# Decay's and rate's first matrices side by side, applied to the input and to the token difference

## The chip, the cores and the metric

The kernel runs on one core of a Trainium2 chip, as one launch. The time is device microseconds of that core, the median of several runs. Engines are named as in the profile: PE is TensorE (PEld its weight loads), DVE is VectorE, ACT is ScalarE, POOL is GpSimd, SP is SyncE, which issues the weight DMAs.

## The reference, cut to what matters

Two layers, an RWKV-7 layer and a differential-attention layer, 512 tokens of width 1024, all in float32. The change touches the beginning of the first layer:

```python
h = rmsnorm(x, norm_g[layer, 0])
h_prev = jnp.pad(h[:, :-1], ((0, 0), (1, 0), (0, 0)))
dx = h_prev - h
xw = h + dx * mix[1]
xa = h + dx * mix[4]
xg = h + dx * mix[5]
...
w_log = -jax.nn.softplus(-(w0 + jnp.tanh(xw @ w1) @ w2)) - 0.5     # decay
a = jax.nn.sigmoid(a0 + (xa @ a1) @ a2)                              # rate
g = jax.nn.sigmoid(xg @ g1) @ g2                                     # gate
```

`w1` and `a1` are 1024 x 64, `g1` is 1024 x 160. Since the mixing vectors act on the 1024 input channels, `xw @ w1` is the same sum as `h @ w1 + dx @ (mix[1][:, None] * w1)`, and likewise for `a1`.

## The kernel before, in words

Activations lie with channels on partitions: X holds h as 8 tiles (k = 0 to 7) of 128 channels x 512 tokens, the kind V_ of St holds the token difference dx in the same tiles. Every dense product is made of three fp32r matmuls: weights and activations are each split in a high part (a copy rounded to fp32r, made by ACT) and a low part (the rest, a subtraction on DVE for activations and on POOL for weights). For an activation tile k, ACT writes xh (`split_high`, L1333) and DVE then xl (`low`, L1840); for a weight block n, ACT writes whi from the raw weights (`high`, L1326) and POOL wlo (`low`, L461 and L464, in two halves of 128 x 1024 for a full block). PE then runs the three products of a tile, L557 (xh with whi), L558 (xl with whi) and L559 (xh with wlo), into a PSUM bank.

Order at the start, which is written out by hand on each engine and held together by semaphores:

- SP loads x, then the raw weights: block 0 (w1, twice side by side, into slot 0 of wraw), block 1 (a1, twice side by side, slot 1), block 2 (g1, slot 0 again, after block 0's low part is made), block 3 (w2 and a2), then the large squares for K, R and V (L371).
- ACT squares x, PE turns x into channel tiles (L581), ACT copies each to X with its norm gain (L1355), POOL takes the difference of neighbouring tokens (L473, semaphore dx), DVE mixes (`mixes`, L1851: dx times a mixing vector plus h, into a slot of tmp), ACT and DVE split the mixed tile.
- There are six mixed inputs in turn: W (decay), A (rate), G (gate), K, R, V. For each, DVE alternates mix and low part, two mixes ahead. The three first feed `dense_block` 0, 1 and 2 on PE: 24 matmuls for W into bank 0, 24 for A into bank 2, 48 for G into banks 0 and 1.
- Between W and A, DVE computes lambda of the second layer's attention (L1871 to L1875, with an exponential on ACT, L1370).
- ACT takes tanh of rows 0 to 63 of bank 0 after block 0 (L1373), and rows 64 to 127 of bank 2 after G's splits (L1377), splits both (L1381, L1382), takes the sigmoid of G's result (L1385), and then evacuates the eight products with w2 and a2 (L1399), one split of K's mixed input behind each pair. K's first dense product (block 4) follows on PE.
- POOL's queue in that stretch: wlo of block 0, eight differences, wlo of block 1 (L464), of block 2 (L461, L464, which also waits for the end of PE's block 0), of block 3, then the squares.

Semaphores that the prediction speaks of: `h_ready` (a tile of X is written), `dx`, `mix_b` (a mixed tile), `x_hi` and `x_ready` (a tile's high and low part), `w_hi` and `w_lo` (a block's), `pe_step` (one per tile of a dense block), `dense_a` (results that ACT has taken), `lora_rdy`. xh and xl have eight tile slots, used again by each input; `split_high` waits on `pe_step` until the tile's last reader is through.

Of the kernel before, what the change touches and what calls it, by code (L numbers as in the profile page):

```python
# [139 lines left out]
def trunk(nc, x, p, norm_g, mlp_w1, mlp_w2, ple_w_up, ple_w_gate, rwkv_mix, rwkv_w_rkvo, rwkv_w0, rwkv_w1,  # L140
# [5 lines left out]
    with ctx:  # L146
# [4 lines left out]
        def at(name, offset, shape, dtype=F32):  # L151
# [107 lines left out]
            h_ready x_edge mix_b x_hi x_ready acc norm_ps norm_rt dense_a dense_v act_link vec_link pool_link  # L259
            lora_hi lora_rdy g_cum dec exps kk_sq kk_ps kk_rt kk_rs kb_ps kn prep  # L260
            bs_mm nl_raw nl_mask inv_ld inv_lk inv_d tdg
# [15 lines left out]
        def vec(c, v):  # L277
            return PV[:, c, v:v + 1]
# [55 lines left out]
        def _(sp):  # L334
# [8 lines left out]
            def load(n, par, parts):  # L343
                for dst, src in parts:
                    sp.dma_start(dst, src).then_inc(raw[par], 16)
# [4 lines left out]
            def cols(r, w, k=CT):  # L350
                return r[:, 0:k * w].rearrange("p (k n) -> p k n", n=w)
# [3 lines left out]

            load(0, 0, [(cols(r0, P)[:, :, 0:64], w1v), (cols(r0, P)[:, :, 64:128], w1v)])
            load(1, 1, [(cols(r1, P)[:, :, 0:64], a1v), (cols(r1, P)[:, :, 64:128], a1v)])
            slot_free(2)
# [192 lines left out]
        def _(pe):  # L551
# [67 lines left out]
            pe.wait_ge(s.h_ready, 3)  # L619
            dense_block(0, 0, 0, 1, X_W)  # L620
            dense_block(1, 1, 1, 1, X_A)
            pe.wait_ge(s.dense_a, 1)
            dense_block(2, 0, 0, 2, X_G)
# [684 lines left out]
        def _(act):  # L1308
# [43 lines left out]
            act.wait_ge(s.par_ev, 1)  # L1352
            for c in range(CT):
                act.wait_ge(s.x_tr, c + 1)
                A(X[:, c, 4:4 + S], pb[c][:, :], ACT.Copy, scale=vec(c, V_N00)).then_inc(s.h_ready, 1)  # L1355
                if c == 3:
                    high(1, 1, slice(0, 1024), True)

            def mix_high(i, k, free):  # L1360
                act.wait_ge(s.mix_b, 8 * i + k + 1)
                split_high(k, tmp[:, mix_place(i, k), :], None, free)
# [4 lines left out]

            mixes(0, None)
            act.wait_ge(s.lam_s, 1)
            A(lamw[:, 2:4], lamw[:, 0:2], ACT.Exp).then_inc(s.lam_e, 1)  # L1370
            mixes(1, 0)
            act.wait_ge(s.pe_step, 8)
            A(rstd[0:64, :], pb[0][0:64, :], ACT.Tanh).then_inc(s.dense_a, 1)  # L1373
            high(2, 0)
            mixes(2, 8 * 1)
            act.wait_ge(s.pe_step, 16)
            A(rstd[64:128, :], pb[2][64:128, :], ACT.Copy).then_inc(s.dense_a, 1)  # L1377
            high(3, 1, slice(0, 1024))
# [425 lines left out]
        def _(dve):  # L1804
# [37 lines left out]
            def mixes(i, mix):  # L1842

                ahead = 2 if i != 4 else 1

                def mixed(k):
                    if i == 0:
                        dve.wait_ge(s.dx, k + 1)
                    if 8 * i + k - 2 * ahead >= 0:
                        dve.wait_ge(s.x_ready, 8 * i + max(k - 2 * ahead, -1) + 1)  # L1850
                    stt(tmp[:, mix_place(i, k), :], St[:, V_, k, :], vec(k, V_MIX + mix), X[:, k, 4:4 + S], ALU.mult, ALU.add)\  # L1851
                        .then_inc(s.mix_b, 1)
                for k in range(ahead):
                    mixed(k)
                for k in range(CT):
                    if k + ahead < CT:
                        mixed(k + ahead)
                    dve.wait_ge(s.mix_b, 8 * i + k + 1)
                    low(k, tmp[:, mix_place(i, k), :], 8 * i + k)
# [7 lines left out]

            mixes(0, MIX_W)

# [6 lines left out]

            mixes(1, MIX_A)
            mixes(2, MIX_G)
# [513 lines left out]
```

## Time and profile before

| | |
|---|---|
| median of 3 runs | 1600.32 us (1599.81 to 1600.70) |
| profiled execution, its own time | 1600.4 us |
| its span in the trace | 1598.5 us |
| mean granted TensorE clock | 0.977 |
| PE busy | 1494.1 us (93%), 9095 matmuls |
| DVE busy | 741.1 us (46%) |
| ACT busy | 590.8 us (37%) |
| POOL busy | 601.3 us (38%) |

### The profile page before, as it was taken

The page shows a single profiled execution, that of the slowest core. Times are in us where ns is not written, and L with a number is a line of the kernel's source. Part 1 is how long each engine was busy: PE and PEld are TensorE (multiplying, and loading weights), DVE is VectorE, ACT ScalarE, POOL GpSimd, SP SyncE. Part 2 cuts the span into 40 slices and gives each one's busy share as a digit, 9 for nine tenths or more (in the row PEclk, how much of TensorE's full clock was granted, in tenths as well). Part 3 has the DMA queues.
Part 4 walks back from the last instruction along what each step waited for, and adds up shares of the span by engine and source line. Part 5 has one row for each costly group of instructions (what it writes and reads, how often), then busy time and mean ns, then how long its engine had stood idle before and what let it go on. Part 6 is the DMA issues. An engine that isn't in the chain of part 4 may idle for free. (4 is left out here: it accounts for less than half of the span.)

```text
span 1598.5 us, 23571 instructions
## 1 busy us (share of the span) xinstructions
PE 1494.1 (93%) x9095; PEld 1176.7 (74%) x9095; DVE 741.1 (46%) x1148; ACT 590.8 (37%) x928; POOL 601.3 (38%) x326
## 2 busy tenths in 40 slices
PE   3798999888999999999999999979999999999998
PEld 3575677775687888888877677745687888888876
DVE  3874888756744310232046773566453300232143
ACT  4655433545332221233153433267342211232252
POOL 4242332323143444443444243334134443434432
PEclk9898999999999999999999999979999999999999
DMA  5121210031023233233322322110022233233231
GB/s 142 53 79 53 80 53 1 4 114 55 25 82 106 81 104 118 81 103 105 105 87 86 126 84 99 55 53 1 19 87 92 92 105 118 80 105 102 82 106 53
DMA packets 123502, 126.97 MB, mean 79 GB/s; under 512 B 8332, under 2 KB 120204, under 8 KB 123416
## 3 DMA queue, kind: packets, MB, share of 16 engines
q1 hardware_dynamic: 122720, 124.51, 24.0%
q8 instruction: 60, 0.98, 0.3%
q0 software_dynamic: 320, 0.66, 0.2%
q10 hardware_dynamic: 376, 0.61, 0.1%
q14 instruction: 26, 0.21, 0.0%
HBM read 123.64 MB, written 2.12 MB: 79 GB/s over the span
## 5 line engine op out<-in xcount | busy, mean ns | idle before, releaser
L461 POOL TENSOR_TENSOR wlo<-wraw,whi 128x1024 fp32r<-128x1024 f32 x108 | 261.1, 2417 | 812.9 <-ACT whi L1326 786.9
L557 PE MATMUL pb<-xh,whi 128*128 128x512 f32 x1184 | 475.5, 402 | 26.3 <-DVE xl L1840 16.1
L559 PE MATMUL pb<-xh,wlo 128*128 128x512 f32 x1184 | 465.0, 393 | 0.0
L558 PE MATMUL pb<-xl,whi 128*128 128x512 f32 x1184 | 464.8, 393 | 0.0
L557 PEld LDWEIGHTS pb<-xh,whi 128*128 128x128 f32 x1184 | 224.3, 189 | 101.7 <-issue 41.8
L1326 ACT ACTIVATE whi<-wraw 128x2048 fp32r<-128x2048 f32 (+1 forms) x111 | 209.2, 1884 | 224.6 <-PE pb L559 224.5
L464 POOL TENSOR_TENSOR wlo<-wraw,whi 128x1024 fp32r<-128x1024 f32 x111 | 275.1, 2478 | 21.4 <-ACT whi L1326 21.4
L558 PEld LDWEIGHTS pb<-xl,whi 128*128 128x128 f32 x1184 | 224.5, 190 | 47.8 <-issue 3.4
L559 PEld LDWEIGHTS pb<-xh,wlo 128*128 128x128 f32 x1184 | 224.4, 189 | 47.8
L557 PE MATMUL pb<-hid_h,whi 128*128 128x512 f32 x512 | 199.3, 389 | 0.0
L558 PE MATMUL pb<-hid_l,whi 128*128 128x512 f32 x512 | 199.2, 389 | 0.0
L559 PE MATMUL pb<-hid_h,wlo 128*128 128x512 f32 x512 | 199.2, 389 | 0.0
L2156 DVE TENSOR_TENSOR X<-X,pb 128x512 f32<-128x512 f32 x40 | 25.7, 684 | 288.1 <-PE pb L559 288.1
L2188 DVE TENSOR_TENSOR tmp<-pb,rstd 128x512 f32<-128x512 f32 x64 | 41.3, 686 | 208.5 <-PE pb L559 208.0
L1639 ACT ACTIVATE hid_h<-tmp 128x512 f32 (+1 forms) x64 | 39.6, 633 | 251.2 <-DVE tmp L2192 251.2
L557 PEld LDWEIGHTS pb<-hid_h,whi 128*128 128x128 f32 x512 | 96.1, 188 | 20.0
L559 PEld LDWEIGHTS pb<-hid_h,wlo 128*128 128x128 f32 x512 | 96.1, 188 | 19.9
L558 PEld LDWEIGHTS pb<-hid_l,whi 128*128 128x128 f32 x512 | 96.1, 188 | 19.8
L2161 DVE SCALAR_TENSOR_TENSOR xl<-X,PV,xh 128x512 fp32r<-128x512 f32 x48 | 55.8, 1222 | 28.3 <-ACT xh L1335 28.3
L1609 ACT ACTIVATE tmp<-X 128x512 f32<-128x512 f32 x40 | 24.2, 627 | 119.9 <-DVE X L2156 119.9
L1840 DVE TENSOR_TENSOR xl<-tmp,xh 128x512 fp32r<-128x512 f32 x64 | 51.7, 818 | 25.0 <-ACT xh L1333 24.9
L1333 ACT ACTIVATE xh<-tmp 128x512 fp32r<-128x512 f32 x64 | 40.1, 632 | 55.9 <-DVE tmp L1851 28.3
(280 smaller groups left out, 1723.4 us busy)
## 6 DMA issues: line engine op xcount, KB each, us to landing
wraw<-in_mlp_w_dram SPq DMA_DIRECT2D x128, 512.0 KB, 4.3
wraw<-in_rwkv_w_rkvo_dram SPq DMA_DIRECT2D x32, 512.0 KB, 4.3
wraw<-in_ple_w_gate_dram SPq DMA_DIRECT2D x16, 512.0 KB, 4.0
xtok<-in_x_dram SPq DMA_DIRECT2D x8, 512.0 KB, 6.3
wraw<-in_w_k_shared_dram SPq DMA_DIRECT2D x8, 512.0 KB, 4.3
wraw<-in_w_v_shared_dram SPq DMA_DIRECT2D x8, 512.0 KB, 3.9
wraw<-in_diff_w_q_dram SPq DMA_DIRECT2D x8, 512.0 KB, 4.3
wraw<-in_diff_w_o_dram SPq DMA_DIRECT2D x8, 512.0 KB, 4.3
```

Of the source, the lines that this page charges most:

```text
L461: pool.tensor_tensor(wlo[:, par, front], wraw[:, par, front], whi[:, par, front].bitcast(F32), ALU.subtract)
L464: pool.tensor_tensor(wlo[:, par, rng], wraw[:, par, rng], whi[:, par, rng].bitcast(F32), ALU.subtract).then_inc(s.w_lo, 1)
L557: mm(o, wh, ah, start=first, stop=False)
L558: mm(o, wh, al, start=False, stop=False)
L559: return mm(o, wl, ah, start=False, stop=last)
L1326: A(whi[:, par, rng], wraw[:, par, rng], ACT.Copy).then_inc(s.w_hi, 1)
L1333: A(xh[:, k, :], src, ACT.Copy).then_inc(s.x_hi, 1)
L1639: A(hid_h[:, bass.ds(4 * i + 2 * h + m, 1), :], tmp[:, 2 + m:3 + m, :], ACT.Copy)\
L1840: tt(xl[:, k, :], src, xh[:, k, :].bitcast(F32), ALU.subtract).then_inc(s.x_ready, 1)
L2156: tt(X[:, c, 0:S], X[:, c, 0:S] if old is None else old, b, ALU.add).then_inc(sem, 1)
L2161: stt(xl[:, k, :], X[:, k, 0:S], vec(k, gain), xh[:, k, :].bitcast(F32), ALU.mult, ALU.subtract)\
L2188: tt(tmp[:, m, :], pb[2 * h + m][:, :], rstd[:, :], ALU.mult).then_inc(s.dense_v, 1)
```

## The change

The two 64-wide matrices are loaded side by side, [w1 | a1], once into slot 0 and once into slot 1 of wraw. DVE multiplies the second copy in place by the mixing vectors (channels are partitions, so the vector is one number for each partition and tile): two instructions of 128 x 8 x 64, semaphore `w_mix`. ACT makes slot 1's high part after that. The activations that meet them are h itself and dx: X_W now stands for the eight tiles of h, X_A for those of dx. Both passes add into one bank, pb[2], rows 0 to 63 for decay and 64 to 127 for rate. The mixed inputs of W and A are no longer made (16 instructions at L1851); G, K, R and V are mixed as before. ACT splits tile c-1 of h between its copies into X, then the eight tiles of dx. Tanh moves behind G's splits.

```diff
@@ -257,7 +257,7 @@
         names = """gnc_in raw0 raw1 w_hi w_lo pe_step cst_in cst2_in x_in0 x_in1 x_in2 x_in3 rows_in hrows_in x2_in p_in lam_in hot_in
             rel_in bvec_out strip_in out_st x_tr x_sq x_rt x_rs x_dg dx par_tr par_ev small_set gains lam_s lam_e
             h_ready x_edge mix_b x_hi x_ready acc norm_ps norm_rt dense_a dense_v act_link vec_link pool_link
-            lora_hi lora_rdy g_cum dec exps kk_sq kk_ps kk_rt kk_rs kb_ps kn prep
+            w_mix lora_hi lora_rdy g_cum dec exps kk_sq kk_ps kk_rt kk_rs kb_ps kn prep
             bs_mm nl_raw nl_mask inv_ld inv_lk inv_d tdg
             x_unit kv_mm kv_ev bt_mm bt_ev lo_ev vz0 vz1 vb0 vb1 ks_mm ll_ev x5_mm xb_ev t5_mm tt_ev
             z_mm0 z_mm1 z_ev0 z_ev1 u_mm0 u_mm1 u_ev0 u_ev1 grown0 grown1 h_ev0 h_ev1
@@ -353,8 +353,8 @@
             a1v = rwkv_a1[0].rearrange("(k p) n -> p k n", p=P)
             g1v = rwkv_g1[0].rearrange("(k p) n -> p k n", p=P)
 
-            load(0, 0, [(cols(r0, P)[:, :, 0:64], w1v), (cols(r0, P)[:, :, 64:128], w1v)])
-            load(1, 1, [(cols(r1, P)[:, :, 0:64], a1v), (cols(r1, P)[:, :, 64:128], a1v)])
+            load(0, 0, [(cols(r0, P)[:, :, 0:64], w1v), (cols(r0, P)[:, :, 64:128], a1v)])
+            load(1, 1, [(cols(r1, P)[:, :, 0:64], w1v), (cols(r1, P)[:, :, 64:128], a1v)])
             slot_free(2)
             load(2, 0, [(cols(r0, 256)[:, :, 0:128], g1v[:, :, 0:128]),
                         (cols(r0, 256)[:, :, 128:256], g1v[:, :, 32:160])])
@@ -617,9 +617,12 @@
 
 
             pe.wait_ge(s.h_ready, 3)
-            dense_block(0, 0, 0, 1, X_W)
-            dense_block(1, 1, 1, 1, X_A)
-            pe.wait_ge(s.dense_a, 1)
+            for n, x_base in ((N_W1, X_W), (N_A1, X_A)):
+                pe.wait_ge(s.w_lo, n + 1)
+                for k in range(CT):
+                    pe.wait_ge(s.x_ready, x_base + k + 1)
+                    three(pb[2][:, :], n, wslice(n, k * P), xs(k), n == N_W1 and k == 0, n == N_A1 and k == CT - 1)\
+                        .then_inc(s.pe_step, 1)
             dense_block(2, 0, 0, 2, X_G)
 
             pe.wait_ge(s.w_lo, 4)
@@ -1350,30 +1353,35 @@
             A(x_rms, x_ss, ACT.Sqrt, bias=eps_n, scale=1.0 / D).then_inc(s.x_rt, 1)
             high(0, 0, slice(0, 1024), True)
             act.wait_ge(s.par_ev, 1)
-            for c in range(CT):
-                act.wait_ge(s.x_tr, c + 1)
-                A(X[:, c, 4:4 + S], pb[c][:, :], ACT.Copy, scale=vec(c, V_N00)).then_inc(s.h_ready, 1)
-                if c == 3:
+            for c in range(CT + 1):
+                if c < CT:
+                    act.wait_ge(s.x_tr, c + 1)
+                    A(X[:, c, 4:4 + S], pb[c][:, :], ACT.Copy, scale=vec(c, V_N00)).then_inc(s.h_ready, 1)
+                if c:
+                    act.wait_ge(s.h_ready, c)
+                    split_high(c - 1, X[:, c - 1, 4:4 + S], None, None)
+                if c == 6:
+                    act.wait_ge(s.w_mix, 2)
                     high(1, 1, slice(0, 1024), True)
+            for k in range(CT):
+                act.wait_ge(s.dx, k + 1)
+                split_high(k, St[:, V_, k, :], None, 0)
 
 
             def mix_high(i, k, free):
-                act.wait_ge(s.mix_b, 8 * i + k + 1)
+                act.wait_ge(s.mix_b, 8 * (i - 2) + k + 1)
                 split_high(k, tmp[:, mix_place(i, k), :], None, free)
 
             def mixes(i, free):
                 for k in range(CT):
                     mix_high(i, k, free)
 
-            mixes(0, None)
+            high(2, 0)
             act.wait_ge(s.lam_s, 1)
             A(lamw[:, 2:4], lamw[:, 0:2], ACT.Exp).then_inc(s.lam_e, 1)
-            mixes(1, 0)
-            act.wait_ge(s.pe_step, 8)
-            A(rstd[0:64, :], pb[0][0:64, :], ACT.Tanh).then_inc(s.dense_a, 1)
-            high(2, 0)
             mixes(2, 8 * 1)
             act.wait_ge(s.pe_step, 16)
+            A(rstd[0:64, :], pb[2][0:64, :], ACT.Tanh).then_inc(s.dense_a, 1)
             A(rstd[64:128, :], pb[2][64:128, :], ACT.Copy).then_inc(s.dense_a, 1)
             high(3, 1, slice(0, 1024))
             act.wait_ge(s.dense_a, 2)
@@ -1844,9 +1852,7 @@
                 ahead = 2 if i != 4 else 1
 
                 def mixed(k):
-                    if i == 0:
-                        dve.wait_ge(s.dx, k + 1)
-                    if 8 * i + k - 2 * ahead >= 0:
+                    if k >= 2 * ahead or i > 2:
                         dve.wait_ge(s.x_ready, 8 * i + max(k - 2 * ahead, -1) + 1)
                     stt(tmp[:, mix_place(i, k), :], St[:, V_, k, :], vec(k, V_MIX + mix), X[:, k, 4:4 + S], ALU.mult, ALU.add)\
                         .then_inc(s.mix_b, 1)
@@ -1855,7 +1861,7 @@
                 for k in range(CT):
                     if k + ahead < CT:
                         mixed(k + ahead)
-                    dve.wait_ge(s.mix_b, 8 * i + k + 1)
+                    dve.wait_ge(s.mix_b, 8 * (i - 2) + k + 1)
                     low(k, tmp[:, mix_place(i, k), :], 8 * i + k)
 
             def lora_low(dst, high, src, r):
@@ -1865,7 +1871,14 @@
                 if z.stop:
                     ts(dst[z], src[z], 0.0, None, ALU.mult).then_inc(s.lora_rdy, 1)
 
-            mixes(0, MIX_W)
+            dve.wait_ge(s.raw1, 32)
+            for m, mix in ((0, MIX_W), (1, MIX_A)):
+                w = wraw[:, 1, 0:CT * P].rearrange("p (k c) -> p k c", c=P)[:, :, 64 * m:64 * m + 64]
+                tt(w, w, PV[:, :, V_MIX + mix:V_MIX + mix + 1].to_broadcast([P, CT, 64]), ALU.mult).then_inc(s.w_mix, 1)
+            for k in range(CT):
+                low(k, X[:, k, 4:4 + S], k)
+            for k in range(CT):
+                low(k, St[:, V_, k, :], CT + k)
 
             dve.wait_ge(s.lam_in, 16)
             link(tt(lrow[:, 0:2, :], lrow[:, 0:4:2, :], lrow[:, 1:4:2, :], ALU.mult))
@@ -1874,7 +1887,6 @@
             link(tt(lamf, lamw[:, 2:3], lamw[:, 3:4], ALU.subtract))
             link(ts(lamf, lamf, LAMBDA_INIT, None, ALU.add))
 
-            mixes(1, MIX_A)
             mixes(2, MIX_G)
             dve.wait_ge(s.lora_hi, 4)
             lora_low(lora_l[:, 0, :], lora_h[:, 0, :], rstd[:, :], slice(0, 64))
```

DVE at the start, from the constants' last instruction to the third mix of G. Before (tmp<-St,PV,X is a mix, xl a low part):

```order
L1831 TENSOR_SCALAR small<-small 128x1
L1851 SCALAR_TENSOR_TENSOR tmp<-St,PV,X 128x512 x3
L1840 TENSOR_TENSOR xl<-tmp,xh 128x512
L1851 SCALAR_TENSOR_TENSOR tmp<-St,PV,X 128x512
...
L1840 TENSOR_TENSOR xl<-tmp,xh 128x512 x3
L1871 TENSOR_TENSOR lrow<-lrow 128x128
L1872 TENSOR_REDUCE small<-lrow 128x2
```

Now:

```order
L1839 TENSOR_SCALAR small<-small 128x1
L1877 TENSOR_TENSOR wraw<-wraw,PV 128x8x64 x2
L1848 TENSOR_TENSOR xl<-X,xh 128x512 x8
L1848 TENSOR_TENSOR xl<-St,xh 128x512 x8
L1884 TENSOR_TENSOR lrow<-lrow 128x128
L1885 TENSOR_REDUCE small<-lrow 128x2
L1887 TENSOR_TENSOR small<-small 128x1
L1888 TENSOR_SCALAR small<-small 128x1
L1857 SCALAR_TENSOR_TENSOR tmp<-St,PV,X 128x512 x3
```

The sixteen mixes of W and A are gone, two products on the weights stand in front, all sixteen low parts come ahead of lambda's four small instructions, and G's mixes follow those.

ACT in the same stretch, from the last copy into whi before the tiles to the lambda exponential. Before:

```order
L1326 ACTIVATE whi<-wraw 128x1024
L1355 ACTIVATE X<-pb,PV 128x512 x4
L1326 ACTIVATE whi<-wraw 128x1024
L1355 ACTIVATE X<-pb,PV 128x512 x4
L1333 ACTIVATE xh<-tmp 128x512 x8
L1370 ACT_TABLE_LOAD
```

Now, from the second copy of slot 1's weights on (ahead of it stand seven copies into X with a split behind each from the second on):

```order
L1329 ACTIVATE whi<-wraw 128x1024
L1359 ACTIVATE X<-pb,PV 128x512
L1336 ACTIVATE xh<-X 128x512 x2
L1336 ACTIVATE xh<-St 128x512 x8
L1329 ACTIVATE whi<-wraw 128x2048
L1381 ACT_TABLE_LOAD
```

Slot 1's high part has moved from behind the fourth copy to behind the seventh, and block 2's (128x2048) from behind A's splits and tanh to ahead of lambda's exponential.

## Rows read from the trace of the kernel before

**Rows 1.** The page: PE's busy time over the whole span.
```profile
PE 1494.1 (93%) x9095; PEld 1176.7 (74%) x9095; DVE 741.1 (46%) x1148; ACT 590.8 (37%) x928; POOL 601.3 (38%) x326
```

**Rows 2.** Stages: start:end, length, busy us by engine, clock, DMA share, GB/s.
```profile
32.40:44.00 11.60, 8.42 (x24) 5.58 (x24) 11.23 (x17) 4.64 (x7) 3.51 (x2) 0.71 0.17 47
...
46.70:55.20 8.50, 7.96 (x24) 4.85 (x24) 8.46 (x14) 5.39 (x8) 0.00 (x0) 0.80 0.01 2
55.20:61.20 6.00, 0.12 (x1) 0.02 (x1) 6.00 (x4) 1.72 (x4) 5.19 (x2) 0.80 0.00 0
61.20:74.30 13.10, 13.09 (x49) 10.62 (x50) 9.52 (x16) 8.40 (x12) 2.40 (x1) 0.83 0.34 108
74.30:92.25 17.95, 14.77 (x50) 10.31 (x48) 14.58 (x17) 16.14 (x27) 6.08 (x2) 0.81 0.30 97
```

**Rows 3.** Timeline of DVE at the start: start us, us, instruction, idle before.
```profile
22.55 0.15 DVE L1831 TENSOR_SCALAR small<-small 128x1 f32<-128x1 f32 x1
...
27.31 1.51 DVE L1851 SCALAR_TENSOR_TENSOR tmp<-St,PV,X 128x512 f32<-128x512 f32 x1 [0.93 <-POOL St L473]
...
33.63 2.83 DVE L1840 TENSOR_TENSOR xl<-tmp,xh 128x512 fp32r<-128x512 f32 x1
```

**Rows 4.** The eight differences on POOL (ns), then POOL's timeline.
```profile
L473 POOL TENSOR_TENSOR St<-X x8: 1032/1094/1483, 22.8 to 31.7; 128x512 f32<-128x512 f32 x8
...
25.86 7.29 POOL L473 TENSOR_TENSOR St<-X 128x512 f32<-128x512 f32 x6 [0.27 <-ACT X L1355]
33.12 2.78 POOL L464 TENSOR_TENSOR wlo<-wraw,whi 128x1024 fp32r<-128x1024 f32 x1
```

**Rows 5.** Timeline of ACT at the start.
```profile
26.58 1.05 ACT L1326 ACTIVATE whi<-wraw 128x1024 fp32r<-128x1024 f32 x1
27.52 1.84 ACT L1355 ACTIVATE X<-pb,PV 128x512 f32<-128x512 f32 x3
...
30.15 1.66 ACT L1333 ACTIVATE xh<-tmp 128x512 fp32r<-128x512 f32 x3
```

**Rows 6.** Timeline from W's last low parts to A's first matmul.
```profile
40.84 1.88 DVE L1840 TENSOR_TENSOR xl<-tmp,xh 128x512 fp32r<-128x512 f32 x3
...
43.90 2.08 DVE L1851 SCALAR_TENSOR_TENSOR tmp<-St,PV,X 128x512 f32<-128x512 f32 x3
...
46.72 0.47 PE L557 MATMUL pb<-xh,whi 128*128 128x512 f32 x1 [2.71 <-DVE xl L1840]
```

**Rows 7.** Timeline where block 2's split meets G's mixes.
```profile
53.35 1.90 ACT L1326 ACTIVATE whi<-wraw 128x2048 fp32r<-128x2048 f32 x1
...
54.14 4.17 DVE L1851 SCALAR_TENSOR_TENSOR tmp<-St,PV,X 128x512 f32<-128x512 f32 x3
...
55.33 2.43 POOL L461 TENSOR_TENSOR wlo<-wraw,whi 128x1024 fp32r<-128x1024 f32 x1 [19.42 <-PE pb L559]
57.73 2.79 POOL L464 TENSOR_TENSOR wlo<-wraw,whi 128x1024 fp32r<-128x1024 f32 x1
...
61.21 0.77 PE L557 MATMUL pb<-xh,whi 128*128 128x512 f32 x1 [5.89 <-DVE xl L1840]
```

**Rows 8.** Timeline of ACT behind G: table load, then the wait for G's product.
```profile
71.53 1.28 ACT L1385 ACT_TABLE_LOAD   x1
74.47 1.09 ACT L1385 ACTIVATE St<-pb 128x512 f32<-128x512 f32 x2 [1.66 <-PE pb L559]
```

**Rows 9.** Timeline of PE in G: two starts at either clock.
```profile
61.77 0.63 PE L558 MATMUL pb<-xl,whi 128*128 128x512 f32 x1
62.20 0.63 PE L559 MATMUL pb<-xh,wlo 128*128 128x512 f32 x1
...
72.00 0.39 PE L559 MATMUL pb<-xh,wlo 128*128 128x512 f32 x1
72.23 0.39 PE L557 MATMUL pb<-xh,whi 128*128 128x512 f32 x1
```

**Rows 10.** DMA in 17 to 19 us, by fortieths: GB/s.
```profile
GB/s 67 67 62 36 36 36 41 21 0 0 0 0 0 0 0 0 0 0 0 0 0 0 0 0 0 0 0 0 0 0 0 0 0 0 0 0 0 0 0 0
```

## The prediction

> **What bounds the kernel now.** I read the page first: PE is busy 1494.1 of 1598.5 us [rows 1], so over the whole span PE decides, and its matmul count does not change here (24 + 24 before, 8 x 3 twice now). What remains are PE's gaps, and the table of stages shows where they are: in the stage of W (32.4 to 44.0) PE is busy 8.4 of 11.6 us and DVE 11.2; in A's (46.7 to 55.2) DVE 8.46 of 8.50; from 55.2 to 61.2 PE stands still and DVE is busy for all six [rows 2]. Until G's product begins at 61.21 the bound is DVE's chain. From there PE (13.1 us of 13.1 in G), then ACT (16.1 of 17.95 in the stage of w2 and a2, up to the start of K at 92.25) [rows 2]. Everything behind runs at distances set by G's beginning, weight loads included, which are released by semaphores of the blocks before. So the gain is how much earlier G's first matmul comes, plus or minus what the G stage itself does otherwise.
>
> The second thing to see is that a DVE instruction's busy time holds waits. A mix that ran while POOL took differences lasted 1.51 us, a low part that met POOL's wlo 2.83 [rows 3], where three low parts in a row, undisturbed, take 1.88, or 0.63 each [rows 6]. The 2.83 us end at 36.46, just after POOL's instruction (33.12 + 2.78 = 35.90) [rows 3, 4]. Likewise three mixes of 2.08 us [rows 6] took 4.17 beside POOL's first half [rows 7]. I take it that DVE gets one instruction in between two of POOL's.
>
> **The DVE chain, before and now.** Removed: 16 mixes at 2.08 / 3 = 0.69 us, 11.1 us of DVE. Added: two products on the weights; the trace has none of the shape 128 x 8 x 64. Bounds: the undisturbed 512-element 0.63 [rows 6] and the disturbed 1.51 [rows 3] each; I take 0.65, disturbed by the first difference, since both have 512 elements a partition. Their data is there: the last of the loads for blocks 0 and 1 trickles out by about 17.4 us [rows 10], the products can start at 22.7, behind the constants [rows 3]. The number of low parts and of splits stays. Without collisions the net would be 11.1 - 1.3 = 9.8, but the low parts now meet POOL in other places, so I go through it in order of time.
>
> 1. Products, 22.75 to 24.9: 0.65, one difference of 1.03 in between (its minimum [rows 4]), 0.65. The second difference then ends at 25.9, the first low part of h at 26.5.
> 2. From here low parts of h and differences alternate. POOL's longest difference is 1.48 us against 1.03 alone [rows 4], and a DVE instruction that met one took 1.51 [rows 3], so I take 1.48 a pair. The differences end at 25.9 + 6 x 1.48 = 34.8, in place of 33.1 [rows 4]; low part 6 is through at 35.4.
> 3. ACT isn't the bound there: from 26.58, two splits at 0.55, four copies at 0.61, five splits and the 1.05 us for the weights make 1.1 + 2.5 + 2.8 + 1.05, to 34.0 [rows 5]. The wait for the products, in front of copy 7 and all later splits, is over at 24.9 and costs nothing; if it were not, those would queue behind it.
> 4. POOL's low part of block 1 runs 34.8 + 2.8 = 37.6 [rows 4] and blocks h's last low part, which ends at 38.2. PE does the tile and frees it at 39.0. ACT has seven splits of dx behind it by then, makes the eighth (39.65) and block 2's high part, 1.90 [rows 7], to 41.55. In the kernel before that came at 53.35: POOL's work on block 2, 2 x 2.4 us, starts 14 us sooner and now falls on the low parts of dx, not on G's mixes.
> 5. Low parts of dx from 38.2 at 0.63: six are through at 42.0. Then POOL's first half to 44.4, one low part to 45.0, second half to 47.4, the last low part to 48.0.
> 6. Lambda: from 42.72 to 43.90 before, 1.2 us [rows 6]; now to 49.2. The table load lies in ACT's wait.
> 7. G's first matmul comes 46.72 - 43.90 = 2.8 us behind its first mix [rows 6]: at **52.0**, in place of 61.21 [rows 7]. That is 9.2 us.
>
> PE costs nothing on the way: the pass over h is paced by the low parts, and that over dx, at worst 24 x 0.43 = 10.3 us [rows 9] from 39.0, is through at 49.3, before G. The same two halves of POOL hide nothing now that they did not before; were the mixes of G late, they would collide again as in rows 7, for 4.2 us.
>
> **G and behind.** DVE's and ACT's order within G is that of before, but tanh (about 0.57 us, priced as the 512-element copies at 0.6) now stands behind the last split. ACT's table load ended at 72.81 and then ACT waited 1.66 us for PE [rows 8], so the tanh is hidden, with 1.1 us to spare, which is also all that a faster G could give. G's product took 13.1 us for 48 matmuls at a granted clock of 0.83 [rows 2], about ten of them 0.43 us apart, the rest 0.23 [rows 9]. The idle time ahead of it falls from 6.0 [rows 2] to some 3 us, so the slow part may be shorter, as ahead of A (clock 0.80 in 8.5 us). I put 0.3 us on that. Sum: 9.2 + 0.3 = 9.5. From the profiled execution's 1600.4 (the median of the runs, 1600.3, is the same) this gives **1590.8**.
>
> **A rule against the row.** The row says that POOL's difference grew by 0.45 us when it met DVE, not by DVE's whole 0.63 [rows 4]. The Trainium skill (SBUF — State Buffer, section "Who interferes with whom") says that a DVE instruction with two SBUF inputs and a GpSimd instruction that reads SBUF exclude each other for the whole instruction. Rows 3 agree for DVE. Taken strictly a pair in step 2 lasts 1.03 + 0.63 = 1.66, not 1.48: six pairs are 1.1 us longer, G begins at 53.1, and the time would be 1591.9. I stay with 1.48, which the rows show.
>
> **Rivals.**
> - *Collisions worse than drawn* (1592.5 to 1597). Each further meeting of DVE with a half of POOL's wlo costs up to 2.2 us (2.83 - 0.63), and one product at 1.51 instead of 0.65 0.9. If G's mixes meet both halves after all, 4.2 us go back: 1595. For it: DVE's last low parts and POOL's second half are 0.6 us apart in my sum. Chance 0.18.
> - *Milder collisions* (1584 to 1589). With none at all, h's low parts follow ACT to 34.6, dx's end at 39.6, ACT's order (dx's last split, block 2's 1.90 us, table load) holds lambda until about 42, G begins at 45: 16 us, 1584. Against it: every meeting in rows 3 and 7 blocked. Chance 0.13 for over 11.5 us.
> - *Nothing arrives at the end*: the earlier G is taken back in a stage that is held by something else, such as the loads. For it I find nothing: behind G the waits are on ACT and PE. Or the passes over h and dx start no earlier because w_mix comes late; the rows of the DMA speak against it. Chance 0.07, within 3.2 us of 1600.3.
> - *Slower, by PE's clock*. The rows show the lower level (1.2 GHz) after each pause: in W, A, G [rows 2], with 0.43 us a matmul in place of 0.23 [rows 9]. Now PE's first passes are sparser, 24 matmuls spread over some nine us. If it stayed at the lower level through G (48 x 0.43 = 20.6 in place of 13.1: +7.5) and the first block of K (48 x 0.2 = +9.6), the sum would be 17.1 - 9.5 = 7.6 us slower, 1608. It decides from about 48 further matmuls at the lower level. Against it: in G the clock came back within 13.1 us at a mean of 0.83. The Trainium skill (TensorE: Matmul & The Clock Gate, Part 1) states that the slow state is the default and that activity releases it. The rows agree; no row shows such sparse work as will stand ahead of G. Chance 0.04.
>
> **How the numbers follow.** Forecast (gain 7.8 to 11.5 us, 1589 to 1592.5) 0.58; worse collisions 0.18; milder 0.13; nothing 0.07; slower 0.04. What a measurement of this kernel can tell from no change is 0.2%, 3.2 us, below 1597.1. Faster therefore 0.58 + 0.13 + 0.18 = 0.89, same 0.07, slower 0.04. The range 1586.5 to 1595.5 takes in the forecast, nearly all of the 4.2 us of a second collision plus the product's 0.9, and a third of the way to the case without any; outside are about 2 in 10.
>
> **What would show it.** Right: in the trace after, G's first matmul near 52, K's near 82.8, DVE's 16 low parts in a row with those of h 1.4 to 1.7 us apart and one or two of 2.5 us or more; the two products under 1.7 us each; POOL's work on block 2 at about 42 to 47; the stages from K on as long as before. Wrong: the step from h's to dx's low parts after 40, a mix of G beside POOL's L461, a granted clock under 0.75 in G, or a K that begins 9 us sooner in a kernel whose end doesn't.

## The result, and the profile after

The changed kernel takes **1587.74 us** (median of 4 runs, 1585.80 to 1589.57) against 1600.38 us before (median of 4 runs too; of three of them it is 1600.32): a ratio of 0.9918, 95% interval 0.9905 to 0.9932, or 12.6 us less (10.9 to 15.2). The forecast was 1590.8 us, 9.5 us less.

| | before | after |
|---|---|---|
| profiled execution, its own time | 1600.4 us | 1585.8 us |
| span in the trace | 1598.5 us | 1584.0 us |
| PE busy | 1494.1 us | 1486.4 us |
| DVE busy | 741.1 us | 734.9 us |
| G's first matmul | 61.2 us | 49.8 us |
| last product with a2 (K follows) | 91.8 us | 78.7 us |

The table of stages of the changed kernel, as in [rows 2]: the pass over h, the pass over dx, the pause ahead of G, G, the products with w2 and a2, the first blocks of K.

```profile
29.50:37.50 8.00, 5.69 (x24) 3.76 (x23) 8.00 (x6) 7.48 (x14) 7.50 (x5) 1.00 0.01 2
37.50:45.70 8.20, 8.06 (x27) 6.08 (x27) 7.83 (x14) 3.92 (x4) 4.52 (x2) 0.79 0.27 65
45.70:49.70 4.00, 0.00 (x0) 0.00 (x0) 4.00 (x5) 1.89 (x3) 1.45 (x1) 0.96 0.30 93
49.70:62.20 12.50, 12.43 (x48) 9.99 (x48) 9.03 (x15) 8.89 (x13) 2.40 (x1) 0.88 0.18 58
62.20:79.10 16.90, 13.07 (x49) 8.46 (x48) 14.60 (x19) 16.00 (x27) 6.12 (x2) 1.00 0.37 123
```

DVE is busy nearly without a break up to G, as before (8.00 of 8.00, 7.83 of 8.20, 4.00 of 4.00), but the stretch in front of G is 11.4 us shorter. In the pass over h, POOL is busy for 7.5 of 8 us too. That is not as much work as it looks: most of the time one of the two works and the other waits inside its instruction. G took 12.5 us (13.1 before), and the stage of w2 and a2 16.9 (17.95), at a granted clock of 1.00 in place of 0.81.

The timeline of DVE, which answers to [rows 3, 6, 7] (start us, us, instruction, idle before):

```profile
22.50 2.14 DVE L1877 TENSOR_TENSOR wraw<-wraw,PV 128x512 f32<-128x512 f32 x2
24.68 1.41 DVE L1848 TENSOR_TENSOR xl<-X,xh 128x512 fp32r<-128x512 f32 x1
26.39 11.16 DVE L1848 TENSOR_TENSOR xl<-X,xh 128x512 fp32r<-128x512 f32 x7 [0.30 <-ACT xh L1336]
37.47 4.89 DVE L1848 TENSOR_TENSOR xl<-St,xh 128x512 fp32r<-128x512 f32 x8
42.29 0.28 DVE L1884 TENSOR_TENSOR lrow<-lrow 128x128 f32<-128x128 f32 x1
...
43.16 1.69 DVE L1887 TENSOR_TENSOR small<-small 128x1 f32<-128x1 f32 x1 [0.27 <-ACT small L1381]
...
45.07 3.95 DVE L1857 SCALAR_TENSOR_TENSOR tmp<-St,PV,X 128x512 f32<-128x512 f32 x3
```

And POOL's in the same stretch, which answers to [rows 4, 7]:

```profile
25.91 8.31 POOL L473 TENSOR_TENSOR St<-X 128x512 f32<-128x512 f32 x6 [0.37 <-ACT X L1359]
34.18 2.82 POOL L464 TENSOR_TENSOR wlo<-wraw,whi 128x1024 fp32r<-128x1024 f32 x1
41.18 3.65 POOL L461 TENSOR_TENSOR wlo<-wraw,whi 128x1024 fp32r<-128x1024 f32 x1 [4.18 <-ACT whi L1329]
44.80 2.36 POOL L464 TENSOR_TENSOR wlo<-wraw,whi 128x1024 fp32r<-128x1024 f32 x1
```

Read together: seven low parts of h take 11.16 us beside POOL's differences and block 1 (2.82), the eight of dx 4.89 with nothing of POOL between them. POOL's first half of block 2 was due at 41.18, yet it ran only from about 42.4 (it ends at 44.83, and one takes 2.4): the last of DVE's row of low parts went through first. Then it held up a subtraction of a single number per partition for 1.5 us (1.69, where [rows 6] leave 1.2 for all of lambda), and the second half held up G's mixes by 1.9 (3.95 for 2.08).

### The profile page after: what moved, and what is told of

The parts are those of the page before. It is cut to its first block and busy times, and to the rows that moved or that the text cites. A ratio compares the mean times of both kernels' runs of the same rounds, so it can differ in the third digit from the quotient of the medians.

```text
span 1584.0 us, 23537 instructions
## 1 busy us (share of the span) xinstructions
PE 1486.4 (94%) x9095; PEld 1173.5 (74%) x9095; DVE 734.9 (46%) x1134; ACT 589.3 (37%) x928; POOL 604.3 (38%) x326
## 5 line engine op out<-in xcount | busy, mean ns | idle before, releaser
L2269 DVE RECIPROCAL tmp<-tmp 128x512 f32<-128x512 f32 x12 | 40.2, 3347 | 22.6 <-ACT tmp L1720 22.6
L1336 ACT ACTIVATE xh<-tmp 128x512 fp32r<-128x512 f32 x48 | 30.3, 634 | 46.0 <-DVE tmp L1857 19.0
```

The lines of the kernel that those rows point to most:

```text
L1336: A(xh[:, k, :], src, ACT.Copy).then_inc(s.x_hi, 1)
L2269: dve.reciprocal(tmp[:, i % 2, :], tmp[:, i % 2, :]).then_inc(s.qk_rs, 1)
```

## The experiments

There are three theories to tell apart. **The chain**: the change pays because DVE's way to G is shorter, and what DVE and POOL do on operands in SBUF excludes one another, so that the sum of both, not DVE's work alone, sets G's beginning. **The order**: it pays because POOL's work on block 2 moved away from G's mixes. **The clock**: it pays because PE spends less time at the lower level in the first 80 us. And one question stands beside them: whatever G gains, does it reach the end?

For each run the landmarks are G's first matmul, the last product with a2, the last step of the second set's inverse (DVE, inv_t), the last matmul from the group norm's rows (PE, rstd with gn_c) and the first copy of the output. They are the last (for the output the first) start that a tile's view gives, for the changed kernel:

```profile
L559 PE MATMUL pb<-rate_h,wlo x8: 388/393/398, 72.2 to 78.7; 128*128 128x512 f32 x8
L2002 DVE TENSOR_TENSOR inv_t<-inv_t,inv_p x60: 191/366/782, 237.8 to 310.4; 128x30 f32<-128x30 f32 x4, 128x58 f32<-128x58 f32 x4, 128x84 f32<-128x84 f32 x4, 128x108 f32<-128x108 f32 x4
L1047 PE MATMUL pb<-rstd,gn_c x16: 587/640/692, 391.2 to 404.7; 32*128 32x512 f32 x16
L1807 ACT ACTIVATE OT<-pb x8: 579/614/654, 1574.9 to 1578.2; 128x512 f32<-128x512 f32 x8
```

| run | G begins | a2 ends | inverse | norm rows | output | median (before, same chip) |
|---|---|---|---|---|---|---|
| before | 61.2 | 91.8 | 325.7 | 419.2 | 1589.4 | 1600.38 |
| before again | 61.2 | 91.5 | 323.7 | 417.5 | 1587.6 | 1601.12 (1601.56) |
| changed | 49.8 | 78.7 | 310.4 | 404.7 | 1574.9 | 1587.74 |
| changed again | 50.0 | 79.5 | 311.6 | 406.3 | 1576.2 | 1588.06 (1601.34) |
| no product | 49.9 | 80.5 | 314.5 | 407.6 | 1578.5 | 1590.14 (1601.34) |
| block 2 cut | 46.5 | 75.6 | 307.8 | 402.8 | 1574.0 | 1585.08 (1601.34) |
| mixes back | 61.4 | 91.8 | 324.9 | 420.4 | 1591.5 | 1600.39 (1601.42) |
| lambda late | 49.2 | 79.2 | 312.8 | 408.3 | 1579.7 | 1590.20 (1601.42) |
| differences on DVE | 48.5 | 77.9 | 309.6 | 406.8 | 1576.6 | 1587.44 (1601.42) |
| all on DVE | 45.6 | 75.6 | 309.4 | 407.3 | 1577.3 | 1587.77 (1601.42) |
| all on DVE again | 45.7 | 75.8 | 309.3 | 404.8 | 1576.2 | 1587.68 (1601.56) |
| idle matmuls ahead of G | 49.9 | 78.3 | 311.0 | 405.7 | 1575.9 | 1587.21 (1601.56) |
| differences and weights on DVE | 46.9 | 77.3 | 309.6 | 405.1 | 1576.4 | 1587.72 (1601.56) |
| all on DVE, idle matmuls later | 45.6 | 75.6 | 309.1 | 404.8 | 1576.1 | 1587.69 (1600.04) |

**The two kernels once more** (no edit).

> The changed kernel itself once more, to see its spread (1585.8 to 1589.6 in four runs, two near 1586 and two near 1589.4) and another profile. If the spread is TensorE's clock, the trace has the same first 80 us (G's first matmul at 49.8, K's at about 79) and the difference of up to 3.5 us comes later, in stretches where the granted clock is at its lower level in one trace and not in the other. If the spread came from DVE and POOL meeting differently, G's first matmul itself would lie up to 3.5 us later.

> The kernel before once more, for a second profile and its spread on this chip: between 1597.5 and 1604. G's first matmul at 61.0 to 61.5 as in the first profile. If TensorE's clock is drawn anew in each execution, the stretches at the lower level behind 200 us lie elsewhere than in the first profile, and K's first matmul comes at 91.5 to 93 all the same.

Measured: the changed kernel 1588.06 (1585.88 to 1589.67), ratio 0.9919, as the first time; the kernel before 1601.12 (1598.62 to 1605.10), ratio 1.0003 to itself. The landmarks up to G agree within 0.2 us between two profiles of one kernel; behind it they differ by 0.3 to 2.0 us. So the place where the spread arises is behind G, and a difference of under 2 us between two profiles at the later landmarks proves nothing. The lead of 11.2 to 11.4 us at G is firm; the lead at the output is 14.5, 13.2, 12.7 or 11.4 us, depending on which two profiles are paired.

**Mixes back on DVE.**

```diff
-            for k in range(CT):
-                low(k, X[:, k, 4:4 + S], k)
-            for k in range(CT):
-                low(k, St[:, V_, k, :], CT + k)
+            for m in range(2):
+                for k in range(CT):
...
+                    stt(tmp[:, k % 4, :], St[:, V_, k, :], vec(k, V_MIX + MIX_W), X[:, k, 4:4 + S], ALU.mult, ALU.add)\
+                        .then_inc(s.extra, 1)
+                    low(k, X[:, k, 4:4 + S] if m == 0 else St[:, V_, k, :], CT * m + k)
...
```

> The changed kernel with sixteen mixes put back on DVE, one ahead of each low part of h and of dx; their results go into tmp, where nothing reads them. Theory (DVE's chain ahead of G decides, together with what POOL does on the same operands): 16 at 0.69 us, less what now falls into waits, plus collisions, so G's first matmul comes 9 to 14 us later, at 59 to 64, and the time is 1597 to 1602. Rival (the gain came from POOL's work on block 2 being moved away from G's mixes): 2 to 4 us later. Rival (TensorE's clock in the first 80 us made the gain): no more than 3 us.

G's first matmul came at 61.36 and the median was 1600.39 us, ratio to before 0.9996 (0.9987 to 1.0005). The work that the change took from DVE, put back with nothing else undone, takes back all of the gain. The chain theory stands. The order theory falls: here too block 2's work was away from G's mixes (POOL at 46.8 to 53.0, G's mixes from 58.5), and nothing was gained. It met a mix and a low part of the pass over dx instead, for the same price of 4.2 us (2.85 + 2.82 for 0.74 + 0.68). The clock theory allowed no more than 3 us, and 12.7 came back. DVE's rows while POOL takes its differences, and where it meets block 2:

```profile
24.97 1.52 DVE L1883 SCALAR_TENSOR_TENSOR tmp<-St,PV,X 128x512 f32<-128x512 f32 x1
26.42 1.52 DVE L1848 TENSOR_TENSOR xl<-X,xh 128x512 fp32r<-128x512 f32 x1
27.87 1.52 DVE L1883 SCALAR_TENSOR_TENSOR tmp<-St,PV,X 128x512 f32<-128x512 f32 x1
...
39.11 0.74 DVE L1883 SCALAR_TENSOR_TENSOR tmp<-St,PV,X 128x512 f32<-128x512 f32 x1
39.78 0.68 DVE L1848 TENSOR_TENSOR xl<-X,xh 128x512 fp32r<-128x512 f32 x1
...
47.97 2.85 DVE L1883 SCALAR_TENSOR_TENSOR tmp<-St,PV,X 128x512 f32<-128x512 f32 x1
50.74 2.82 DVE L1848 TENSOR_TENSOR xl<-St,xh 128x512 fp32r<-128x512 f32 x1
```

And POOL's first half of block 2:

```profile
46.83 3.44 POOL L461 TENSOR_TENSOR wlo<-wraw,whi 128x1024 fp32r<-128x1024 f32 x1 [9.45 <-ACT whi L1329]
```

The starts are 1.45 us apart beside the differences and 0.65 alone: the two engines take turns, one instruction each, and a turn of both costs 0.2 us less than the 0.63 + 1.03 of the two alone.

**Without the products** (decay and rate then take dx unmixed; the line put in is shown shortened).

```diff
-                tt(w, w, PV[:, :, V_MIX + mix:V_MIX + mix + 1].to_broadcast([P, CT, 64]), ALU.mult).then_inc(s.w_mix, 1)
+                dve.memset(small[:, 178 + m:179 + m], 0.0).then_inc(s.w_mix, 1)
```

> The changed kernel without the two products on the weights, so decay and rate take dx unmixed; two memsets of one element stand in their place. The products took 2.14 us of DVE in the trace, one difference of POOL in between. Theory: h's low parts are paced by ACT's splits and POOL's differences, so of the 2.14 us only 0.5 to 1.5 reach G's first matmul (48.3 to 49.3). If the products were wholly on the path, it would be 47.6.

G began at 49.86, so the products cost nothing there: my 0.5 to 1.5 us was too much. DVE then waits for ACT's splits, and POOL's differences end at the same time:

```profile
24.56 1.11 DVE L1848 TENSOR_TENSOR xl<-X,xh 128x512 fp32r<-128x512 f32 x1 [2.07 <-ACT xh L1336]
...
27.97 9.68 DVE L1848 TENSOR_TENSOR xl<-X,xh 128x512 fp32r<-128x512 f32 x6 [0.59 <-ACT xh L1336]
37.58 4.89 DVE L1848 TENSOR_TENSOR xl<-St,xh 128x512 fp32r<-128x512 f32 x8
```

The low parts of dx begin at 37.58, with the products at 37.47. The median was 2.1 us above that of the changed kernel for all that, and G's beginning doesn't explain it: the last product with a2 came 1.0 to 1.8 us later, in the stretch behind G. The trace shows what was different there. In this profile PE's granted clock was 0.81 in the stage of w2 and a2, where both profiles of the changed kernel have 1.00, and ACT, which sets the pace of that stage, waited twice for PE. In the kernel before, at 0.81 too, it waited 0.82 and 0.78 us at the same two places; in neither profile of the changed kernel does it wait for PE there.

```profile
72.03 1.27 ACT L1407 ACTIVATE St<-pb,PV 128x512 f32<-128x512 f32 x2 [0.83 <-PE pb L559]
...
74.59 1.27 ACT L1407 ACTIVATE St<-pb,PV 128x512 f32<-128x512 f32 x2 [0.78 <-PE pb L559]
```

**Block 2's low part cut to 8 elements** (the gate's first product then lacks the low part of its weights; POOL fills the upper half of that slot with zeros once, early on).

```diff
+            pool.memset(wlo[:, 0, 1024:2048].bitcast(F32), 0.0)
             low(0, 0, slice(0, 1024), True)
...
-            low(2, 0, slice(0, 2048), False)
+            low(2, 0, slice(0, 8), False)
```

> The changed kernel with POOL's low part of block 2 cut to 8 of its 2048 elements a partition, so the gate's first product lacks that part. In the trace this work met lambda's small instructions (1.69 us for one of 0.16) and G's mixes (3.95 us for three of 2.08), 3.4 us in all. Theory: G's first matmul comes 3.2 to 3.5 us sooner, at 46.3 to 46.6, and the time is 3 us lower plus or minus the clock's spread. Rival (DVE would have waited there for something else, ACT's splits or lambda's exponential): under 1.5 us.

G began at 46.46, 3.3 us sooner, and the median fell by 3.0 us to 1585.08. Lambda's subtraction is back at 0.16 us and the three mixes at 2.08:

```profile
43.25 0.16 DVE L1888 TENSOR_TENSOR small<-small 128x1 f32<-128x1 f32 x1 [0.27 <-ACT small L1382]
...
43.63 2.08 DVE L1858 SCALAR_TENSOR_TENSOR tmp<-St,PV,X 128x512 f32<-128x512 f32 x3
```

The meeting with POOL's two halves is worth what the rows said, 3.4 us, and nearly all of it (3.3) lies on the path to G. How much of it reaches the end is less sure: at the output this profile is ahead of the two of the changed kernel by 0.9 and 2.2 us, and the intervals of the two ratios (0.9885 to 0.9916 and 0.9906 to 0.9933) overlap.

**Lambda late.** Its sum stands behind G's low parts, its exponential ahead of the decays, the rest behind the scans.

```diff
+            mixes(2, MIX_G)
             dve.wait_ge(s.lam_in, 16)
...
-            dve.wait_ge(s.lam_e, 1)
-            link(tt(lamf, lamw[:, 2:3], lamw[:, 3:4], ALU.subtract))
-            link(ts(lamf, lamf, LAMBDA_INIT, None, ALU.add))
-
-            mixes(2, MIX_G)
...
+            dve.wait_ge(s.lam_e, 1)
+            link(tt(lamf, lamw[:, 2:3], lamw[:, 3:4], ALU.subtract))
+            link(ts(lamf, lamf, LAMBDA_INIT, None, ALU.add))
```

> The changed kernel with lambda's four small instructions taken out from between dx's low parts and G's mixes: the sum goes behind G's low parts, its exponential ahead of the decays, the rest behind the scans. In the trace they stand from 42.29 to 45.03, of which 1.2 us are their own and 1.5 a wait on POOL's block 2. Theory of two engines that exclude each other (DVE and POOL instructions with two inputs in SBUF run one at a time, so that the sum of both decides): only the 1.2 us go, the wait moves on to G's mixes, and G's first matmul comes at 48.4 to 48.8. If the wait goes too, it comes at 47.0.

G began at 49.19: 0.6 us sooner, less than the 1.2 us of lambda's own work. DVE's mixes, then POOL's halves:

```profile
42.14 6.30 DVE L1857 SCALAR_TENSOR_TENSOR tmp<-St,PV,X 128x512 f32<-128x512 f32 x3
```

```profile
41.02 3.44 POOL L461 TENSOR_TENSOR wlo<-wraw,whi 128x1024 fp32r<-128x1024 f32 x1 [4.18 <-ACT whi L1329]
44.42 2.80 POOL L464 TENSOR_TENSOR wlo<-wraw,whi 128x1024 fp32r<-128x1024 f32 x1
```

The three mixes now hold both waits, 6.30 - 2.08 = 4.2 us, where lambda and mixes together held 3.4: part of lambda (a reduction, and the wait for ACT) had lain beside POOL for nothing. Moving work away from a collision moved the collision. The median, 1590.20, is 2 us worse than the changed kernel's (the intervals of the ratios, 0.9917 to 0.9948 and 0.9906 to 0.9933, overlap); as without the products, what was lost lies behind G.

**The differences on DVE.**

```diff
-                pool.tensor_tensor(St[:, V_, k, :], X[:, k, 3:3 + S], X[:, k, 4:4 + S], ALU.subtract).then_inc(s.dx, 1)
...
             for k in range(CT):
+                dve.wait_ge(s.h_ready, k + 1)
...
+                tt(St[:, V_, k, :], X[:, k, 3:3 + S], X[:, k, 4:4 + S], ALU.subtract).then_inc(s.dx, 1)
                 low(k, X[:, k, 4:4 + S], k)
```

> The changed kernel with the eight differences on DVE (0.63 us each in a row) instead of POOL (1.03 us each), each ahead of the low part of its tile of h. DVE gets 5.0 us more work. Theory of exclusion: DVE and POOL take turns anyway, so the sum of both falls by 8 x 0.4 = 3.2 us; ACT's splits hold some of it back: G's first matmul 0.5 to 3 us sooner, at 47 to 49.3. Rival (DVE alone is the bound and POOL's part is beside it): 3 to 5 us later, at 53 to 55.

DVE got 5 us more work and G began 1.3 us **sooner**, at 48.50. The rival, DVE alone as the bound, is out by 4.5 us or more. The products, with no difference between them, now take 1.29 us in place of 2.14, and up to the low parts of dx only the one that meets POOL's block 1 is long:

```profile
22.32 1.29 DVE L1872 TENSOR_TENSOR wraw<-wraw,PV 128x512 f32<-128x512 f32 x2
...
31.02 0.69 DVE L1843 TENSOR_TENSOR xl<-X,xh 128x512 fp32r<-128x512 f32 x1
...
32.63 2.48 DVE L1843 TENSOR_TENSOR xl<-X,xh 128x512 fp32r<-128x512 f32 x1 [0.32 <-ACT xh L1331]
```

**The weights' low parts on DVE too**, with lambda in its place, and with lambda late (twice).

```diff
-            low(1, 1, slice(0, 1024), True)
-            low(2, 0, slice(0, 2048), False)
+            for m in range(2):
+                pool.wait_ge(s.w_dve, m + 1)
+                pool.memset(small[:, 180 + m:181 + m], 0.0).then_inc(s.w_lo, 1)
...
+                    tt(wlo[:, 0, 0:1024], wraw[:, 0, 0:1024], whi[:, 0, 0:1024].bitcast(F32), ALU.subtract)
+                    tt(wlo[:, 0, 1024:2048], wraw[:, 0, 1024:2048], whi[:, 0, 1024:2048].bitcast(F32), ALU.subtract)\
+                        .then_inc(s.w_dve, 1)
...
+            tt(wlo[:, 1, 0:1024], wraw[:, 1, 0:1024], whi[:, 1, 0:1024].bitcast(F32), ALU.subtract).then_inc(s.w_dve, 1)
```

> The kernel with the differences and the low parts of weight blocks 1 and 2 on DVE, but lambda back in its place between dx's low parts and G's mixes. Theory: as nothing of POOL is left in the way, lambda costs its own 1.2 us: G's first matmul at 46.5 to 47.0 (45.56 with lambda late). The time within 2 us of the changed kernel's, below it if the clock behind 200 us allows.

> As the kernel with the differences on DVE, with lambda late, and also the low parts of weight blocks 1 and 2 on DVE, three halves at some 1.2 us in place of 2.4 on POOL (POOL passes their signal on with a one-element memset each). Theory of exclusion: the sum falls by 3.2 + 3 x 1.2 + 1.2 = 8 us, of which ACT's order (dx's last split and block 2's high part, to 41 us) leaves about half: G's first matmul at 45.5 to 47, the time 2.5 to 4 us below the changed kernel. Rival: DVE becomes the bound with its 8.6 us more and G begins later than 50.

> The kernel with everything on DVE and lambda late, once more: its G began 4.2 us sooner than the changed kernel's, but its median was the same, 4 us of its lead being lost between 300 and 413 us, where TensorE's lower level showed. If that is a draw of each execution, the second profile loses another amount there and the median comes out 1 to 3 us below the changed kernel's (1585 to 1587). If it is a property of this kernel's timing, the loss of 3 to 4 us stands there again and the median stays at 1587.5 to 1588.5.

G began at 46.92 with lambda in place and at 45.56 and 45.74 with lambda late. All three lie where the exclusion theory put them (46.5 to 47.0, 45.5 to 47), with DVE doing 5.0 + 3 x 1.2 us more than in the changed kernel. Lambda costs 1.2 to 1.4 us once POOL isn't in the way, against 0.6 beside it. A half of a weight block takes 1.22 us on DVE:

```profile
41.80 1.22 DVE L1860 TENSOR_TENSOR wlo<-wraw,whi 128x1024 fp32r<-128x1024 f32 x1
42.93 1.22 DVE L1861 TENSOR_TENSOR wlo<-wraw,whi 128x1024 fp32r<-128x1024 f32 x1
```

But the medians, 1587.72, 1587.77 and 1587.68, are the changed kernel's 1588.06 within its spread. Of a lead of 4.2 us over the changed kernel at G, some 3 are left at the last product with a2, 1 to 2 at the inverse, and at the group norm and the output it is gone or lies within the spread of two profiles (table). My expectation of 2.5 to 4 us less at the end was wrong. The second profile lost 2.4 us less between inverse and norm rows than the first, but 1.4 more behind them, so the large loss at that place was one execution's, and the missing gain is not.

**The clock ahead of G.**

```diff
+            pe.wait_ge(s.h_ready, CT)
+            for j in range(6):
+                mm(pb[6][:, 0:384], ident, cst[:, 0:384], start=True, stop=True)
             dense_block(2, 0, 0, 2, X_G)
```

> The changed kernel with six idle matmuls of 128 x 384 in float32 (about 0.64 us each, into a bank that nothing reads) in the pause between the pass over dx and G. Theory: G then runs at the upper level from its first matmul, 1.0 to 1.7 us less for its 48, but ACT waits only 0.50 us for G's end in the trace, so K's first matmul comes at most 0.5 us sooner (78.2 to 79.5 in place of 78.7 and 79.5) and the time is the same within its spread. Rival (G's clock was worth its whole 1.7 us): K at 77.0 to 77.8.

G's granted clock was 1.00 in place of 0.88:

```profile
49.80:61.60 11.80, 11.12 (x48) 8.94 (x48) 8.34 (x14) 8.53 (x13) 2.40 (x1) 1.00 0.18 64
```

The last product with a2 came at 78.3, 0.4 us ahead of the changed kernel's first profile and 1.2 of its second. ACT, whose wait for G had been 0.50 us, has none left. So G's clock is worth 0.4 to 1.2 us up to K; the rival's 1.7 us did not come. The median of four runs is 1587.21; one of the four took 2980 us, for which no trace shows a cause, and the ratio is taken without it.

**The clock between 300 and 400 us.** In the first profile of the kernel with everything on DVE, PE's granted clock was 0.66 from 380 to 390 us, in the changed kernel's first profile 1.00 (0.83 in its second); the same pair of sums took 2.07 us in one and 1.13 in the other. First the former, stage and instruction, then the latter:

```profile
380.00:390.00 10.00, 8.99 (x27) 3.90 (x28) 6.58 (x7) 0.74 (x2) 0.41 (x1) 0.66 0.33 107
```

```profile
381.01 2.07 PE L1005 MATMUL pb<-tmp,cst 128*128 128x512 f32 x2 [1.64 <-DVE tmp L2088]
```

```profile
380.00:390.00 10.00, 8.56 (x42) 5.15 (x42) 8.31 (x8) 2.31 (x5) 0.70 (x1) 1.00 0.33 107
```

```profile
381.30 1.13 PE L1009 MATMUL pb<-tmp,cst 128*128 128x512 f32 x2 [1.65 <-DVE tmp L2080]
```

So I filled those pauses:

```diff
             for c in range(CT):
+                for j in range((0, 0, 0, 1, 2, 1, 2, 1)[c]):
+                    spin(2, 384)
                 bonus(c)
```

> The kernel with everything on DVE and lambda late, and seven idle matmuls of 128 x 384 in the pauses of PE among the bonus sums (0.7 to 1.7 us each, at 372 to 386 us in the first profile), where the granted clock fell to the lower level and 3 us of the lead went. Theory (the lead is given back by the clock in the sparse stage between 300 and 413 us): no lower level from 370 to 395, the lead over the kernel before at 413 us is within 1.5 us of that at 300, and the median is 1 to 2.5 us under 1587.7. Rival (the lead is lost to waits of DVE and ACT in that stage): the same median as without them, or the idle matmuls' own time on top, 1 to 3 us.

No stretch at the lower level between 370 and 395, and the way from inverse to norm rows took 95.7 us in place of 97.9; but the second profile without the idle matmuls, which has 1.00 from 380 to 390 by itself, took 95.5 there, and the median stayed at 1587.69. The rival's "same median" is what came. The clock explains the one bad stretch of that profile, not why the kernels that start G earlier end no earlier.

## Why the prediction was right, and where its sizes were off

- *DVE's chain up to G is the bound, and the gain is G's earlier start*: right. G 11.4 us sooner; the mixes put back bring 61.4 and the old time.
- *Steps 1 and 2*: the products ended at 24.6 (24.9 forecast, though 22.75 and the step's own terms add up to 25.1) and the six differences took 8.31 us, 1.39 a pair, where I took 1.48 and the strict rule 1.66. That they stand on the path was wrong: without them G began at the same time. The Trainium skill (SBUF — State Buffer, "Who interferes with whom") says that a DVE instruction with two SBUF inputs and a GpSimd instruction that reads SBUF exclude each other. The runs with work moved between the two engines agree that they hold each other up (5 us more on DVE, G 1.3 us sooner). That they do so for the whole of both instructions did not come out: a pair took 0.27 us less than the 1.66 us of the two alone.
- *Steps 3 and 4*: right within 0.7 us. Copies and splits were not the bound, dx's low parts began at 37.5 (38.2), block 2's high part ended at 41.1 (41.55).
- ***Step 5* is the one that failed**: "one low part" between POOL's halves, and dx's low parts through at 48.0. They were through at 42.3: POOL's first half, due when two of the eight were not yet through, waited 1.3 us until they were done. The meeting came in lambda and in G's mixes after all, which I had only as a rival, and it cost 3.4 us in place of the 4.8 in my sum. That is 1.4 us; with 0.7 us from step 4 and 0.1 of rounding it makes the 2.2 us between 52.0 and 49.8.
- *Steps 6 and 7*: 1.2 us for lambda is its own work; beside POOL it costs 0.6, alone 1.2 to 1.4.
- *G and behind, 0.3 us*: too small. The lead grew from 11.4 at G to 13.1 at the last product with a2 (from 11.2 to 12.0 between the second profiles). G itself gave some 0.6 of the first (12.5 us for 13.1), the rest is the stage of w2 and a2, which ran at 0.81 before [rows 2] and at 1.00 after, and in which ACT no longer waits for PE. My sum did not price that stage.
- *The end*: the leads at the output scatter from 11.4 to 14.5 us over pairs of profiles. 12.6 measured, against 9.5: 2.2 us from steps 4 and 5, the rest from behind G. (1600.4 less 9.5 is 1590.9, not 1590.8.)
- *Rivals*: the collision of G's mixes with block 2 did happen, and still the time was better than forecast, since it replaced the other collision instead of adding to it. The slow clock did not come: 1.00 over h, 0.79 over dx, 0.88 in G. "Nothing arrives at the end" came true not for this change but for the 4 us beyond it.

What stays open is why a G that begins at 45.6 instead of 49.8 ends no earlier. The profiles say where the lead goes, and that PE's clock stood lower where it went. From G to the last product with a2 the five profiles with a granted clock of 0.93 to 0.95 took 28.4 to 29.5 us, those at 0.89 30.0 to 30.1, those at 0.81 to 0.85 30.3 to 30.6. From there to the inverse six profiles at 0.96 took 233.5 to 234.0 us, the other eight, at 0.97 or 0.98, 231.7 to 233.1. All three profiles with everything on DVE and lambda late are at 0.89 and 0.96, both of the changed kernel at 0.93 or more and 0.97, and this is 2 to 3 of the 4.2 us. Whether an earlier G brought the lower clock or something else did isn't shown: lambda late did the same to both stretches with a G at 49.2, and with lambda in place only the first was slow (30.4 us at 0.85), yet the median is the same. The rest goes between the inverse and the group norm's rows (94.3 and 94.7 us in the changed kernel, 95.5 to 97.9 with everything on DVE) and, in two of the three, behind them; for this no cause is shown.

## What to carry to other kernels

Before counting an engine's busy time as its work, look at the same instruction in an undisturbed place: 0.63 us against 1.4 to 2.8 here showed that two engines were sharing one road. Where DVE and GpSimd both work on pairs of SBUF tensors, add their times (here 1.39 to 1.45 us a pair, of 1.66); work moved from the slower to the faster of the two shortens the chain even if that engine is already "full". And weigh an early gain at several landmarks downstream: two profiles of the same kernel differed by up to 2 us behind 80 us, so a lead smaller than that can't be claimed from one pair of traces, and a larger one can still vanish.

## What the runs showed of the hardware that I had not expected

- A POOL instruction that came due while DVE was in a row of its own did not always get in after the one DVE instruction in work. It waited 1.3 us (3.65 for 2.4) in the changed kernel, over two low parts, and 1.1 us (3.44) over two DVE instructions with the mixes back and with lambda late; in the kernel before it came in without a wait (2.43, [rows 7]). Once both had work in hand they took turns. What decides between these no run shows.
- A DVE subtraction of one number per partition waits like a large one: 1.69 us for 0.16.
- The spread of one kernel is 4 to 6.5 us (1585.9 to 1589.7; before 1598.6 to 1605.1), while up to G, in the first 50 to 60 us, two profiles agree within 0.2.
- The same kernel stage ran at quite different granted clocks: 0.81 and 1.00 for the products with w2 and a2 in kernels with the same work there, and the lower one cost ACT two waits of 0.8 us.
